# Turning three quarters of the FFN tokens and both mixer latents by VectorE and DRAM instead of TensorE

## The reference, cut to what matters

```python
h = rms_norm(x, attn_norm_w)                         # x: 256 tokens x 2048, f32
hq, hf, hi, hg, c_q, c_kv, k_r = split(h @ w_in)     # c_q, c_kv: the two latents, 512 wide each; k_r: 64
q  = rms_norm(c_q,  q_norm_w)  @ w_uq                # latents -> 8 heads x 192
kv = rms_norm(c_kv, kv_norm_w) @ w_ukv
o_a = hgrn2_mixer(hq, hf, hi, hg, ...)               # gated linear recurrence, 8 heads
o_b = attention(rope(q), rope(k), v)                 # rope needs cos/sin of the positions
x = x + concat([o_a, o_b]) @ w_out
h = rms_norm(x, ffn_norm_w)
gate, up = split(h @ w_gate_up)                      # 2048 -> 2 x 5632
x = x + (silu(gate) * up) @ w_down
```

## Time and profile before

| what | value |
|---|---|
| median of 3 runs | 1108.22 us (1107.96 to 1108.38) |
| the profiled execution: its time, its span | 1107.74 us, 1106.0 us |
| PE busy | 1096.4 us, 99% of the span |
| DVE busy | 903.1 us, 82% |
| ACT busy | 645.8 us, 58% |
| POOL busy | 65.2 us, 6% |
| chain that ended last | PE 97%, DVE 1%, the rest 0% each |
| granted TensorE clock | 1.00 all through |

### The profile page before, as it was taken

How to read it: one execution, slowest core, us unless ns; L and a number is a source line. 1 busy time by engine, 2 the same in 40 slices (tenths; PEclk the granted TensorE clock), 3 DMA queues, 4 the chain that set the end, 5 groups by cost and what they waited for, 6 DMA issues and landing times.

```text
span 1106.0 us, 15243 instructions
## 1 busy us (share of the span) xinstructions
PE 1096.4 (99%) x5126; PEld 922.6 (83%) x5126; DVE 903.1 (82%) x1249; ACT 645.8 (58%) x907; POOL 65.2 (6%) x164
## 2 busy tenths in 40 slices
PE   8999999999999999999999999999999999999998
PEld 8988888888888878888888888888888888888887
DVE  6688787587876587688888988988988889999887
ACT  6676776668654466365455455554554555654553
POOL 1500000000000010001101101001011010000000
PEclk9999999999999999999999999999999999999999
DMA  8966455554645486766777777777777777666665
GB/s 305 289 186 206 129 169 166 151 160 155 229 171 187 155 239 194 229 220 210 248 231 223 240 232 222 230 234 217 235 236 226 239 264 236 218 214 206 197 202 171
DMA packets 108083, 234.21 MB, mean 212 GB/s; under 512 B 8448, under 2 KB 17408, under 8 KB 107776
## 3 DMA queue, kind: packets, MB, share of 16 engines
q1 hardware_dynamic: 101360, 211.34, 59.2%
q0 software_dynamic: 6528, 22.03, 6.9%
q10 hardware_dynamic: 144, 0.20, 0.1%
HBM read 221.99 MB, written 11.53 MB: 211 GB/s over the span
## 4 chain that ended last, share of the span: by engine, by line
PE 97%; DVE 1%; ACT 0%; issue 0%; DMA 0%; DVEq 0%; ACTq 0%
PE side L2029 24%; PE main L1798 22%; PE side L2031 12%; PE main L1801 11%; PE side L1999 4%; PE side L2000 4%; PE side L2001 4%; PE main L2001 3%; PE main L2000 3%; PE main L1999 3%; PE main L1818 2%; PE side L1924 1%; PE side L1840 0%; PE side L1875 0%; PE side L1876 0%
## 5 line engine op out<-in xcount | busy, mean ns | idle before, releaser
L1048 ACT CAST w_hi<-raw 128x1024 fp32r<-128x1024 f32 x245 | 240.2, 986 | 157.2 <-PE side L2029 80.3
L1637 DVE TENSOR_TENSOR w_lo<-raw,w_hi 128x1024 fp32r<-128x1024 f32 x245 | 274.6, 1133 | 15.1 <-ACT w_hi L1048 15.0
L1159 DVE TENSOR_TENSOR w_lo<-raw,w_hi 128x1024 fp32r<-128x1024 f32 (+3 forms) x156 | 178.8, 1155 | 93.4 <-ACT w_hi L826 91.8
L826 ACT CAST w_hi<-raw 128x1024 fp32r<-128x1024 f32 (+3 forms) x155 | 153.5, 999 | 125.1 <-PE main L1798 111.3
L1798 PE MATMUL main<-w_hi,hT_hi 128*128 128x512 f32 (+2 forms) x416 | 160.9, 388 | 0.0
L1801 PE MATMUL main<-w_hi,hT_lo 128*128 128x512 f32 (+2 forms) x416 | 157.6, 380 | 0.0
L2029 PE MATMUL side<-w_hi,hT_hi 128*128 128x512 f32 x400 | 155.6, 389 | 0.0
L2031 PE MATMUL side<-w_hi,hT_lo 128*128 128x512 f32 x400 | 155.6, 389 | 0.0
L1798 PE MATMUL main<-w_lo,hT_hi 128*128 128x512 f32 (+2 forms) x416 | 107.1, 379 | 0.0
L2029 PE MATMUL side<-w_lo,hT_hi 128*128 128x512 f32 x400 | 106.9, 389 | 0.0
L1801 PEld LDWEIGHTS main<-w_hi,hT_lo 128*128 128x128 f32 x416 | 78.2, 188 | 13.0
(11 more groups left out here) (305 smaller groups left out, 1882.8 us busy)
## 6 DMA issues: line engine op xcount, KB each, us to landing
raw<-in_w_gate_up SPq DMA_DIRECT2D x176, 512.0 KB, 4.9
raw<-in_w_down SPq DMA_DIRECT2D x88, 512.0 KB, 4.4
raw<-in_w_in SPq DMA_DIRECT2D x64, 512.0 KB, 4.3
raw<-in_w_out SPq DMA_DIRECT2D x32, 512.0 KB, 3.7
raw<-in_w_in SPq DMA_DIRECT2D x15, 384.0 KB, 5.5
squares<-hiddenT POOLq DMA_DIRECT2D x11, 512.0 KB, 4.7
hiddenT<-squares POOLq DMA_DIRECT2D x44, 128.0 KB, 5.5
raw<-in_w_ukv SPq DMA_DIRECT2D x8, 512.0 KB, 4.4
```

Source lines behind the costliest of these rows:

```text
L826: copy(w_hi[:, slot, 0:n], raw[:, slot, 0:n]).then_inc(s_hi, 1)
L1048: copy(w_hi[:, n % RING, 0:cols], src).then_inc(s_hi, 1)
L1159: tt(w_lo[:, slot, 0:n], raw[:, slot, 0:n], w_hi[:, slot, 0:n].bitcast(F32), ALU.subtract)\
L1637: tt(w_lo[:, n % RING, 0:cols], src, w_hi[:, n % RING, 0:cols].bitcast(F32), ALU.subtract)\
```

## The change: what it does

1. **Latents.** `lat_t` goes. `lat_turn` (DVE) transposes the 32x32 blocks of a whole latent in one 128x1024 instruction, at positions 23 and 27; SP writes them to a new DRAM scratch behind the loads of granules 31 and 36 and reads them back, four pieces of 128 KB, behind the loads of 33 and 38; `lat_back` splits them at positions 30 and 34, ahead of `kr_b`.
2. **FFN tokens.** Chunk 2 goes by DRAM too; only chunk 3 stays with PE, and its `x2` moves from position G0+2 to G0. `FF_ORDER` becomes 0, 3, 1, 2. SP issues chunk 0's two transfers (behind the loads of G0+1 and G0+2), POOL those of chunks 1 and 2, one chunk after the other. `x_back` stands at G0-1, G0+2 and G0+4.
3. **Additions.** `out2`'s addition and `x_turn` move one position earlier, so DVE does them ahead of the next conversion and not behind it.
4. **Angles and sines** move to positions 14 and 15, in the second block of latent columns. The positions are loaded behind granule 12 with a semaphore of their own, and `angles` waits for fewer of POOL's constants.

```diff
-FF_ORDER = [(c, n) for c in (2, 0, 1, 3) for n in range(2)]
+FF_ORDER = [(c, n) for c in (0, 3, 1, 2) for n in range(2)]
+POS_AFTER = 12
+LAT_OUT_AFTER = (31, 36)
+LAT_BACK_AFTER = (33, 38)
...
-        s += [(e + 1, ("lat_a", i)), (e + 2, ("lat_b", i))] + [(e + 5, ("lat_t", i, n)) for n in range(2)]
+        s += [(e + 1, ("lat_a", i)), (e + 2, ("lat_b", i)), (e + 2, ("lat_turn", i))]
+        s += [((30, 34)[i], ("lat_back", i, n)) for n in range(2)]
     e = END[("lat", 2)]
-    s += [(e + 1, ("kr_a",)), (e + 4, ("angles",)), (e + 5, ("sines",)), (e + 9, ("kr_b",))]
+    s += [(e + 1, ("kr_a",)), (14, ("angles",)), (15, ("sines",)), (e + 9, ("kr_b",))]
...
     for c in range(4):
-        s += [(END[("out1", c)], ("out1", c)), (END[("out2", c)], ("out2", c)), (END[("out2", c)] + 1 + (c == 2), ("sq2", c))]
+        s += [(END[("out1", c)], ("out1", c)), (END[("out2", c)] - 1, ("out2", c)), (END[("out2", c)] + 1, ("sq2", c))]
     e = END[("out2", 3)]
-    s += [(END[("out2", c)], ("x_turn", c)) for c in range(2)]
-    s += [(e + 2 * c, ("x_back", c, n)) for c in range(2) for n in range(2)]
-    s += [(e - 1 if c == 2 else e + 2, ("x2", c, n)) for c in range(2, 4) for n in range(2)]
+    s += [(END[("out2", c)] - 1, ("x_turn", c)) for c in range(3)]
+    s += [((e - 1, e + 2, e + 4)[c], ("x_back", c, n)) for c in range(3) for n in range(2)]
+    s += [(e, ("x2", 3, n)) for n in range(2)]
...
+                if g in LAT_OUT_AFTER:
+                    i = LAT_OUT_AFTER.index(g)
+                    sp.wait_ge(s_latturned, i + 1)
+                    sp.dma_start(lat_scratch[i].rearrange("a c b x -> (a c) b x"), latents_in_blocks[i])\
+                        .then_inc(s_latout[i], 16)
+
+                if g in LAT_BACK_AFTER:
+                    i = LAT_BACK_AFTER.index(g)
+                    sp.wait_ge(s_latout[i], 16)
+                    for b in range(P // Q):
+                        sp.dma_start(latents_in_blocks[i][Q * b:Q * (b + 1), :, :],
+                                     lat_scratch[i][:, :, b, :].rearrange("a c x -> c a x")).then_inc(s_latback[i], 16)
...
+                if j == 1:
+                    x_out(sp, 0)
+                if j == 2:
+                    x_back(sp, 0)
...
+                elif kind == "lat_turn":
+                    i = a[0]
+                    dve.wait_ge(s_lat, NT * (i + 1))
+                    nc.vector.transpose(latents_in_blocks[i].rearrange("p b (n r) -> p n b r", r=Q),
+                                        latents[i][:, :, :].rearrange("p t (k b c) -> p (t k) b c", b=P // Q, c=Q))\
+                        .then_inc(s_latturned, 1)
+                elif kind == "lat_back":
+                    i, j = a
+                    dve.wait_ge(s_latback[i], MOVED)
+                    dve.wait_ge(s_thi, SPLIT[s] + 1)
+                    src = latents_in_blocks[i].rearrange("p a (t k r) -> p k t a r", t=NT, r=Q)
+                    for k in (2 * j, 2 * j + 1):
+                        col = (V_KVN if i else V_QN) + k
+                        for t in range(NT):
+                            hi, lo = [v[:, 4 * i + k, t * P:(t + 1) * P].rearrange("p (a r) -> p a r", r=Q)
+                                      for v in (mT_hi, mT_lo)]
+                            ins = stt(out=lo, in0=src[:, k, t, :, :], scalar=vec_cols[:, col:col + 1],
+                                      in1=hi.bitcast(F32), op0=ALU.mult, op1=ALU.subtract)
+                    ins.then_inc(s_tlo, 1)
```

More of the change, by code:

```diff
@@ L302, in side_uses @@
     kind = step[0]
-    if kind in ("x2", "lat_t", "o_t"):
+    if kind in ("x2", "o_t"):
         return [(step, "dve")]
@@ L327 @@
             GIVEN[USE[_key]] = _given[_engine]
-SPLITS = [step for _, step in SCHEDULE if step[0] in ("x", "x2", "x_back", "lat_t", "o_t", "attend")]
+SPLITS = [step for _, step in SCHEDULE if step[0] in ("x", "x2", "x_back", "lat_back", "o_t", "attend")]
 SPLIT = {step: n for n, step in enumerate(SPLITS)}
@@ L352, in split_needed @@
     if kind == "uq":
-        return SPLIT[("lat_t", 0, 1)] + 1
+        return SPLIT[("lat_back", 0, 1)] + 1
     if kind == "ukv":
-        return SPLIT[("lat_t", 1, 1)] + 1
+        return SPLIT[("lat_back", 1, 1)] + 1
     if kind == "out1":
@@ L452, in hybrid_layer @@
         latents = (lat, hv)
+        latents_in_blocks = [v[:, :, :].rearrange("p t c -> p (t c)").rearrange("p (a x) -> p a x", a=P // Q)
+                             for v in (hkT, hgate)]
         qTn = X[:, 0, :].rearrange("p (h t) -> p h t", h=HEADS)
@@ L482, in in_blocks @@
         def in_blocks(c):
-            return (hiddenT[:, :, :], all_of(hidden).rearrange("p (a x) -> p a x", a=P // Q))[c]
+            if not c:
+                return hiddenT[:, :, :]
+            return all_of((hidden, gate)[c - 1]).rearrange("p (a x) -> p a x", a=P // Q)
         def turned(t, c=0):
@@ L506, in hybrid_layer @@
         s_small = sem("s_small")
+        s_pos = sem("s_pos")
         s_lbin = sem("s_lbin")
@@ L512, in hybrid_layer @@
         s_lat = sem("s_lat")
+        s_latturned = sem("s_latturned")
+        s_latout = [sem(f"s_latout{i}") for i in range(2)]
+        s_latback = [sem(f"s_latback{i}") for i in range(2)]
         s_sq = sem("s_sq")
@@ L533, in hybrid_layer @@
         s_xturned = sem("s_xturned")
-        s_xout = [sem(f"s_xout{c}") for c in range(2)]
-        s_xback = [sem(f"s_xback{c}") for c in range(2)]
+        s_xout = [sem(f"s_xout{c}") for c in range(3)]
+        s_xback = [sem(f"s_xback{c}") for c in range(3)]
         s_turned = sem("s_turned")
@@ L595, in bank, with x_out, x_back @@
             return side[n % SIDE]
+        def x_out(engine, c):
+            engine.wait_ge(s_xturned, NT * (c + 1))
+            engine.dma_start(x_scratch[c].rearrange("a c b x -> (a c) b x"), in_blocks(c)).then_inc(s_xout[c], 16)
+        def x_back(engine, c):
+            engine.wait_ge(s_xout[c], 16)
+            for b in range(P // Q):
+                engine.dma_start(in_blocks(c)[Q * b:Q * (b + 1), :, :],
+                                 x_scratch[c][:, :, b, :].rearrange("a c x -> c a x")).then_inc(s_xback[c], 16)
         def pick(v, first, *dims):
@@ L625, in hybrid_layer @@
         N_IDENT = 2
+        N_FREQ = 2 + 3 + HALF
         N_CONST = 2 + 3 + 1 + 2 * 3 * LEVELS + 2 + 2 + HALF
@@ L647, in _ @@
                     sp.dma_start(X[:, :, cols], x_v[:, :, cols]).then_inc(s_x[X_AFTER[g]], 16)
+                if g == POS_AFTER:
+                    sp.dma_start(pos_i[:, :], positions[0].rearrange("(t p) -> p t", p=P),
+                                 allow_slow_non_contiguous=True).then_inc(s_pos, 16)
                 if 0 <= g - SMALL_AFTER < N_SMALL:
@@ L768, in _ @@
             pool.dma_start(X[:, :, :], x_v).then_inc(s_xagain, 16)
[L770 to L777, removed]
+            for c in (1, 2):
+                x_out(pool, c)
+                x_back(pool, c)
             def move_out(i):
@@ L902, in step @@
                     root(("lat_a",) + a, NT)
-                elif kind == "lat_t":
+                elif kind == "lat_back":
                     i, j = a
-                    ps, k, col = filled(s), 4 * i + 2 * j, (V_KVN if i else V_QN) + 2 * j
-                    split_hi([(mT_hi[:, k + n, :], ps[:, n * SEQ:(n + 1) * SEQ], col + n) for n in range(2)])
+                    act.wait_ge(s_latback[i], MOVED)
+                    src = latents_in_blocks[i].rearrange("p a (t k r) -> p k t a r", t=NT, r=Q)
+                    split_hi([(mT_hi[:, 4 * i + k, :].rearrange("p (t a r) -> p t a r", t=NT, r=Q), src[:, k, :, :, :],
+                               (V_KVN if i else V_QN) + k) for k in (2 * j, 2 * j + 1)])
                 elif kind == "kr_a":
@@ L957, in step @@
                     if kind == "hq" and not a[0]:
-                        act.wait_ge(s_side, USE[("lat_t", 0, 1)] + 1)
+                        act.wait_ge(s_latturned, 1)
                     if a[0] and kind == "hg":
@@ L1217, in angles @@
             def angles():
-                dve.wait_ge(s_small, 16 * N_SMALL)
-                dve.wait_ge(s_const, N_CONST)
+                dve.wait_ge(s_pos, 16)
+                dve.wait_ge(s_const, N_FREQ)
                 link(nc.vector.tensor_copy(pos_f[:, :], pos_i[:, :]))
@@ L1287, in step @@
                         ts(v, v, inv[:, t:t + 1], None, ALU.mult).then_inc(s_lat, 1)
-                elif kind == "lat_t":
-                    i, j = a
-                    ps, k, col = filled(s), 4 * i + 2 * j, (V_KVN if i else V_QN) + 2 * j
-                    split_lo(s, [(mT_lo[:, k + n, :], ps[:, n * SEQ:(n + 1) * SEQ], mT_hi[:, k + n, :], col + n)
-                                 for n in range(2)])
+                elif kind == "lat_turn":
[4 more added lines that the diff above has]
+                        .then_inc(s_latturned, 1)
+                elif kind == "lat_back":
+                    i, j = a
+                    dve.wait_ge(s_latback[i], MOVED)
```

(8 more changed lines are left out.)

11 lines of the change are left out of this document (6 added, 5 removed).

## The result

The changed kernel takes 1114.02 us (median of 5 runs, 1113.58 to 1114.29) where the kernel before takes 1108.1 beside it: ratio 1.0051, 95% interval 1.0040 to 1.0062. That is 5.9 us slower, and above my range. The profiled execution took 1113.58 us with a span of 1110.6, 4.6 more than the span of before; the rest of the 5.8 us between the two profiled executions, 1.2 us, lies around the span.

The account below looks back on a forecast made before the run. PE was taken to bound the kernel, with 97% of the chain. 1.5 us late at `q_t` less 0.2 won at G0 gave +1.3 on 1107.74, so 1109.0; the median, 0.5 above, 1109.5 us; range 1107.2 to 1112.0.

Parts of the forecast that it names:

- The angles' length: Angles at their new place behind granule 17: 4.8 us on DVE, as at the old place, ending at 40.75.
- Its consequence: Granules 19 to 21: conversions ready after PE is due, 0.8 us lost by then.
- The wait at granule 27: Granule 27 ready at 61.5 with PE due at 60.7, so PE there 0.7 us later than before.
- The kv latent landed late: kv latent's transfers by DRAM: 4.3 us each, last returning piece landing at 83.9, when ACT wants it, 84.0.
- My third rival: kv latent lands late: at 7.3 us a transfer, ACT, DVE's chain and PE 2.9 us later, 1112.4 us; chance 0.22.
- DVE's chain to `q_t`: Behind granule 33: `lat_back` adds 2.19 us, chain ends 16.8 us behind it, new PE wait of 1.7 us.
- the end of the mixer: Around G0: net gain 0.2 us, as a wait of about 1.6 comes before chunk 3's transposes.
- The fourth rival: Table's drain: ACT stands still 1.4 us behind the sine's closing load, delaying granule 19 onward, 1110.9 us; chance 0.05.

Follow-up runs that it names:

- run 1: The changed kernel with POOL's masks made only after DVE has finished the angles: 1111.81 us, ratio 1.0032.
- run 9: The changed kernel with POOL's masks made early, once the input's nine pieces are split, and the load of lower bounds behind them: 1111.67 us, ratio 1.0030.
- run 7: The changed kernel with POOL's masks behind the angles, sines at position 24 and the kv latent's `lat_back` at 38: 1108.53 us, ratio 0.9995.
- run 8: run 7 plus chunk 0's `x_back` ahead of chunk 3's addition, chunk 3's `x2` at G0+1, SP's two transfers one load sooner: 1108.42 us, ratio 0.9993.
- Run 3: The changed kernel with the kv latent's `lat_back` at position 38 instead of 34: 1110.20 us, ratio 1.0019.
- run 4: The changed kernel with latents turned by TensorE again and angles and sines back at 29 and 30: 1108.12 us, ratio 1.0000.
- run 12: The changed kernel with masks early, sines at 24, the kv latent's `lat_back` at 38, and the mixer's end retimed: 1105.78 us, ratio 0.9979.

## Why the prediction was wrong

- **The angles' length failed.** "The angles take 68.74 to 73.52, 4.8 us" was read at their old place and carried to the new one without looking at what POOL does there. They took 6.4. Runs 1 and 9 show the cause. The Trainium skill bears on it ("SBUF — State Buffer", Who interferes with whom): VectorE's second pair of ports is shared with GpSimd, whoever issues first has it for the whole instruction, and casts and `tensor_scalar` can ask for it. The rows agree for these: in the changed kernel the cast and some `TENSOR_SCALAR` grew, in run 7 a pair of `TENSOR_SCALAR` took 2.96 beside memsets, and in run 8 it kept its 0.88 and a memset grew instead (1.67 instead of 1.38). Two other steps, with two inputs each, are not covered by that: the `TENSOR_TENSOR` of the angles grew from 0.29 to 0.43, the six `SCALAR_TENSOR_TENSOR` hardly (1.93 us before, 1.97 after).
- **Its consequence was undersized too.** PE lost 2.6 us from 17 to 21 (3.17 - 0.55), forecast 0.8: the angles are 1.6 longer and began at 36.90, 0.9 behind my 35.96, of which the opening's lag explains 0.55. For angles of 4.8 us the forecast's own sum came out where DVE was as early as I had it: 0.79 in run 1, with the angles 4.22 ahead of granule 17 (forecast 4.39), but 1.52 in run 9, with 3.43. The wait at granule 27 didn't come in the changed kernel, since PE was late already, and stood where it was forecast in run 1.
- **The kv latent landed late.** My third rival named it: ACT would wait if the transfers took over some 4.4 us. I gave it 0.22 and took 4.3. The way out took 6.5, and the last piece of the return 4.6: ACT starts on it 8.3 behind granule 33 (87.67 - 79.41), where its landing was forecast 6.1 behind (83.9 - 77.8). ACT waited 1.2 and DVE 0.98, not the rival's 2.9. The late load of granule 36 added 0.77, for which I had no term. It was issued late, behind DVE's late conversion of granule 32, and landed slowly. By estimate either alone would have been hidden: after 4.3 us it would have been there at 79.1, and ACT would have come to it at 79.7 (78.29 before, and PE 1.37 later). No run tries them apart. In all `q_t` came 18.6 behind granule 33, forecast 16.8; 1.8 us.
- **Right: DVE's chain to `q_t`.** It is the bound there, 2.19 of `lat_back` go into it, and its idle time ahead gives nothing. Run 3 takes them out and the wait is gone.
- **Right: the end of the mixer,** -0.2 (4.82 to 4.61), with a wait of 1.4 where I gave 1.6; run 4 gives 1.000.
- **Right: no drain behind the table load.** Granule 19's conversion starts 0.02 us behind it, after the change as before. The fourth rival is out.
- **Not foreseen: the opening and the time around the span.** PE reached granule 17 at 40.90, ahead of all that was changed but the load of the positions; over the runs it is 40.15 to 40.95, whatever the edit, so I take this 0.55 for scatter of one execution; no run tests it. Around the span the profiled execution had 3.0 us, not 1.7. Kernels with the latents by DRAM had 1.9 to 2.1 in the median (2.5 in the changed kernel's own runs), those without 1.73 to 1.78. What in them makes 0.3 us of it is open.

Sum of the misses in the profiled execution: 0.55 opening, 1.8 early, -0.8 at granule 27, 1.8 at `q_t`, 1.2 around the span: 4.5, on a forecast of 1109.0 for it.

## What to carry to other kernels

A step's duration belongs to its place: before it is moved, read the timelines of all engines there, of GpSimd above all when VectorE's step has casts and `tensor_scalar`. A transfer through DRAM that the engines read in order wants its consumer placed by the slowest landing in the trace, and behind the steps for which PE waits next. Where the change loses, look for the position and not for the idea: with a few steps moved, and the masks, +5.9 us became -2.4, each against the kernel before beside it.

## What the runs showed of the hardware

- With POOL's masks running into the angles, VectorE's 128x2 cast took 0.73 us instead of 0.16 (0.77 beside a memset in run 12; 0.16 beside POOL's issue of a load alone in runs 1 and 9), three of four 128x128 `TENSOR_SCALAR` 0.41 to 0.55 instead of 0.23, and two 128x512 ones beside memsets 2.96 instead of 0.88. It goes both ways: one 128x64 affine select of POOL took 1.27 us in run 7 where its like took 0.24.
- A write of 512 KB to DRAM from SP's queue landed after 5.0 us for one latent and 6.5 for the other, the return in 128 KB pieces after 3.0 to 5.2, in the median 3.4 and 3.5, half of what POOL's pieces took before, in another stretch of the kernel. Granule 36's load of 512 KB took 5.6 there.
